# Combining the expert rows by rank: seven ranks read back and added before the end, the eighth tile by tile

## The reference, cut to what matters

```python
def swiglu(x, w1, w3, w2):
    return (silu(x @ w1) * (x @ w3)) @ w2       # 1024 -> 256 -> 1024

def moe(x, ...):
    scores = sigmoid(x @ w_router)
    idx = top 8 of the biased scores within the best 4 of 8 groups
    gates = 2.5 * scores[idx] / sum(scores[idx])
    return swiglu(x, w1_s, w3_s, w2_s) + sum over the 8 of gate * swiglu(x, w1_e[i], w3_e[i], w2_e[i])

x = layer_norm(ALPHA * x + moe(x), ln3_g, ln3_b)
```

## Time and profile before

| | |
|---|---|
| time of the runs, median of 3 | 1402.59 us (1402.55 to 1405.86) |
| span of the profiled execution | 1401.5 us |
| busy: PE, DVE, ACT, POOL | 1282.4, 495.9, 275.4, 226.2 us |
| the first down product ends, the last ends | 588.5 us, 1320.7 us |
| period of an expert within the loop | 11.76 us |

### The profile page before, as it was taken

One profiled execution on the slowest core, in us unless ns is written; L12 is line 12 of the kernel. 1 busy time (PEld: TensorE's weight loads), 2 busy tenths in 40 slices (PEclk: granted clock), 3 DMA queues, 4 the chain that ended last, 5 costly groups with the idle time before them and its releaser, 6 DMA issues.

```text
span 1401.5 us, 19230 instructions
## 1 busy us (share of the span) xinstructions
PE 1282.4 (92%) x7579; PEld 1009.6 (72%) x7579; DVE 495.9 (35%) x1063; ACT 275.4 (20%) x454; POOL 226.2 (16%) x212
## 2 busy tenths in 40 slices
PE   5999596999979999999999999999999999999651
PEld 4888254868846685788888888888888888888420
DVE  0169998131187348111111111111111111111078
ACT  1125124022235150111111111111111111111100
POOL 2039000000000002011111111111111111111061
PEclk9999798999999999999999999999999999999887
DMA  9330303033155532688888888888888888888193
GB/s 340 152 120 2 134 11 150 1 120 136 59 190 233 181 139 69 246 312 318 321 312 313 315 313 310 306 311 308 312 314 315 312 316 311 308 309 305 41 381 160
DMA packets 75990, 319.12 MB, mean 228 GB/s; under 512 B 14055, under 2 KB 20415, under 8 KB 55941
## 3 DMA queue, kind: packets, MB, share of 16 engines
q1 hardware_dynamic: 57525, 278.60, 53.3%
q0 software_dynamic: 16992, 35.49, 7.0%
q10 hardware_dynamic: 1424, 4.35, 0.8%
HBM read 307.16 MB, written 36.38 MB: 245 GB/s over the span
## 4 chain that ended last, share of the span: by engine, by line
PE 77%; DVE 17%; DMA 2%; issue 1%; ACT 1%; POOL 0%; ACTq 0%; DVEq 0%; POOLq 0%; SPq 0%
PE psum L651 73%; DVE act_mem L1461 7%; PE psum L666 5%; DVE act_mem L1921 2%; DMA act_mem<-in_w_conv_b_dram 1%; DVE mk_mem L1621 1%; DVE act_mem L1529 1%; DVE st L1927 1%; DVE act_mem L1932 0%; DMA arena<-in_w_o_dram 0%; DVE act_mem L1915 0%; DVE act_mem L1559 0%; DVE act_mem L1475 0%; DMA arena<-y_rows 0%; DMA y_rows<-act_mem,idx_y 0%
## 5 line engine op out<-in xcount | busy, mean ns | idle before, releaser
L651 PE MATMUL psum<-act_mem,arena 128*128 128x112 f32 (+1 forms) x5504 | 791.6, 305 | 6.7 <-DMA arena<-in_w_o_dram 3.8
L651 PEld LDWEIGHTS psum<-act_mem,arena 128*128 128x128 f32 x5504 | 736.0, 193 | 52.6 <-DMA arena<-in_w_o_dram 4.6
L651 PE MATMUL psum<-arena,act_mem 128*112 128x512 f32 (+2 forms) x616 | 276.7, 593 | 1.0 <-DVE act_mem L1820 0.9
L651 PEld LDWEIGHTS psum<-arena,act_mem 128*112 128x112 f32 (+2 forms) x616 | 101.5, 174 | 124.5 <-issue 123.7
L570 POOL DMA_INDIRECT y_rows<-act_mem,idx_y x64 | 72.6, 1134 | 616.5 <-DVE idx_x L1814 580.4
L1817 DVE TENSOR_TENSOR act_mem<-act_mem,psum 128x224 f32<-128x224 f32 x64 | 24.8, 388 | 389.9 <-ACT act_mem L1351 389.9
L1820 DVE TENSOR_SCALAR act_mem<-psum,act_mem 112x512 f32<-112x512 f32 x64 | 48.0, 750 | 227.9 <-PE psum L651 227.9
L1351 ACT ACTIVATE act_mem<-psum 128x224 f32<-128x224 f32 x64 | 22.9, 358 | 433.3 <-PE psum L651 433.3
L1461 DVE SCALAR_TENSOR_TENSOR act_mem<-act_mem,wcb 128x511 f32<-128x511 f32 (+29 forms) x90 | 86.9, 1016 | 1.1
L1354 ACT ACTIVATE act_mem<-psum,act_mem 112x512 f32<-112x512 f32 x64 | 44.0, 687 | 164.6 <-PE psum L651 164.6
L666 PE MATMUL psum<-ident,act_mem 112*128 112x112 f32 (+4 forms) x390 | 53.5, 280 | 24.8 <-DMA act_mem<-in_x_sample_dram 10.0
(11 more groups left out here) (221 smaller groups left out, 705.9 us busy)
## 6 DMA issues: line engine op xcount, KB each, us to landing
arena<-in_w_e_dram SPq DMA_DIRECT2D x192, 1024.0 KB, 7.9
arena<-in_w_in_dram SPq DMA_DIRECT2D x16, 512.0 KB, 16.9
arena<-in_cache_mem_k_dram SPq DMA_DIRECT2D x8, 1024.0 KB, 9.1
arena<-in_cache_mem_v_dram SPq DMA_DIRECT2D x8, 1024.0 KB, 11.6
arena<-y_rows SPq DMA_DIRECT2D x8, 1024.0 KB, 12.8
arena<-y_rows SPq DMA_DIRECT2D x4, 1536.0 KB, 8.7
arena<-in_w_v_dram SPq DMA_DIRECT2D x1, 4096.0 KB, 24.3
arena<-in_w_k_dram SPq DMA_DIRECT2D x1, 4096.0 KB, 14.0
```

The lines of the kernel that those rows point to most:

```text
L651: return pe.matmul(out, lhsT, rhs, start=first, stop=last)
```

## The change

Instead of reading whole tiles back after the last expert, the kernel reads the rows of one rank for all 512 prompt tokens, as soon as no expert can write that rank any more. Ranks 0 to 3 are read in two halves of two tiles (`early_in`, one buffer for each half, in memory that the router no longer needs) and added by DVE in steps 61 (rank 0), 62 (ranks 1 and 2) and 63 (rank 3). The read of rank 0 stands on SP's queue ahead of expert 63's weights. Ranks 4, 5 and 6 are read into weight slots 0 to 2, and added by DVE, four tiles in one instruction, after its last scaling. Rank 7 is read tile by tile into slot 3. GpSimd's and PE's sums are gone. The 64 rows of the sample tokens are read at the end, and PE sums them with `sel8`, a 0/1 matrix that GpSimd makes at the start. The order of tiles is 0 to 4, the sample tile last, and the statistics of a tile stand before the norm of the tile before it. As the slow path must start from `base` without these sums, SP stores `base` to DRAM at the start of the experts.

```diff
-LAST_ORDER = [4, 0, 1, 2, 3]
-PARTS = [(0, 3), (3, 5), (5, 7), (7, 8)]
-POOL_ROWS = (1, 4)
-PE_ROWS = [(2,), (3,), (5,), ()]
-DVE_ROWS = [(0,), (), (6,), (7,)]
-SMALL_ROWS = [(0, 2), (3,), (5, 6), (7,)]
+NT = SEQ // P
+EARLY = 4
-        y_in = [arena[:, 8192 * n:8192 * n + 8192].rearrange("p (j n) -> p j n", j=TOPK) for n in range(3)]
+        sel8 = sb("sel8", [NS * TOPK, NS])
+        early_in = [kv_mem[:, 2048:4096].rearrange("p (t n) -> p t n", t=2),
+                    act_mem[:, A3:A3 + 2 * D].rearrange("p (t n) -> p t n", t=2)]
+        late_in = [arena[:, 6144 * n:6144 * n + NT * D].rearrange("p (t n) -> p t n", t=NT) for n in range(TOPK - EARLY)]
+        sample_in = kv_mem[0:NS * TOPK, 2048:2048 + D]
+        y_ranks = y_rows[0:SEQ * TOPK, :].rearrange("(t p j) n -> p t j n", p=P, j=TOPK)
-            with sp.Fori(0, E // 4 - 1) as i:
+            wait_out(sp, "so4")
+            for t in range(TT):
+                w = width(t)
+                sp.dma_start(base_rows[t * P:t * P + w, :], base[0:w, t, :]).then_inc(s_bsave, 16)
+            with sp.Fori(0, E // 4 - 2) as i:
                 for n in range(4):
 
                     sp.wait_ge(m_y, 4 * i + (n + 1))
                     expert(n, 4 * i + (n + 4), s_w[n])
 
+            def rank_written(j):
+
+                e = E - TOPK + j
+                sp.wait_ge(m_s[0], 16 * (e // 2 + 1))
+                sp.wait_ge(m_s[1], 16 * ((e + 1) // 2))
+
+            def early_rank(j):
+
+                rank_written(j)
+                for n in range(2):
+                    if j > 0:
+                        sp.wait_ge(s_added[n], j)
+                    sp.dma_start(early_in[n], y_ranks[:, 2 * n:2 * n + 2, j, :]).then_inc(s_early[n], 16)
+
+            for n in range(4):
+                sp.wait_ge(m_y, E - 8 + n + 1)
+                if n == 3:
+                    wait_out(sp, "so4")
+                    sp.wait_ge(s_table, 1)
+                    early_rank(0)
+                expert(n, E - 4 + n, s_w[n])
+            for j in range(1, EARLY):
+                early_rank(j)
             sp.wait_ge(s_over, 1)
+            n_max = sp.value_load(over[0:1, 0:1], min_val=0, max_val=T)
+            for n in range(TOPK - EARLY - 1):
+                sp.wait_ge(m_y, E - 4 + n + 1)
+                rank_written(EARLY + n)
+                sp.dma_start(late_in[n], y_ranks[:, :, EARLY + n, :]).then_inc(s_late_in[n], 16)
+
             sp.wait_ge(m_y, E)
-            n_max = sp.value_load(over[0:1, 0:1], min_val=0, max_val=T)
             with sp.If(n_max > CAP):
+                sp.wait_ge(s_late_add, TOPK - EARLY - 1)
                 with sp.Fori(1, E * (ROUNDS - 1) + 1) as i:
                     sp.wait_ge(f_sem["it"], i)
                     expert(0, (i - 1) % E, f_sem["w"])
-            for p in range(2):
-                sp.wait_ge(m_s[p], 16 * (E // 2))
-            sp.wait_ge(s_done, 1)
-            for n, t in enumerate(LAST_ORDER):
-                w = width(t)
-                if n >= 3:
-                    sp.wait_ge(s_rowv, n - 2)
-                for q, (j0, j1) in enumerate(PARTS):
-                    sp.dma_start(y_in[n % 3][0:w, j0:j1, :],
-                                 y_rows[t * D:t * D + w * TOPK, :].rearrange("(p j) n -> p j n", j=TOPK)[:, j0:j1, :]).then_inc(
-                        s_yin[q][n % 3], 16)
...
+            rank_written(TOPK - 1)
+            for t in range(NT):
+                sp.dma_start(late_in[3][:, t, :], y_ranks[:, t, TOPK - 1, :]).then_inc(s_last_in[t], 16)
+            sp.wait_ge(s_added[0], EARLY)
+            sp.dma_start(sample_in, y_rows[SEQ * TOPK:NROW, :]).then_inc(s_sample_in, 16)
@@ gpsimd @@
+            gp.memset(sel8[:, :], 1.0).then_inc(s_sel8, 1)
+            gp.wait_ge(s_sel8, 1)
+            gp.affine_select(out=sel8[:, :], in_=sel8[:, :], compare_op=ALU.is_ge, fill=0.0, base=0,
+                             pattern=[[-TOPK, NS]], channel_multiplier=1).then_inc(s_sel8, 1)
+            gp.wait_ge(s_sel8, 2)
+            gp.affine_select(out=sel8[:, :], in_=sel8[:, :], compare_op=ALU.is_ge, fill=0.0, base=TOPK - 1,
+                             pattern=[[TOPK, NS]], channel_multiplier=-1).then_inc(s_sel8, 1)
...
-            for n, t in enumerate(LAST_ORDER):
-                w = width(t)
-                rows_in = y_in[n % 3][0:w]
-                gp.wait_ge(s_yin[0][n % 3], 16 * (n // 3 + 1))
-                gp.tensor_tensor(rows_in[:, 0, :], rows_in[:, 0, :], rows_in[:, POOL_ROWS[0], :], ALU.add).then_inc(s_ypool, 1)
-                gp.wait_ge(s_ypool, 2 * n + 1)
-                gp.wait_ge(s_yin[1][n % 3], 16 * (n // 3 + 1))
-                gp.tensor_tensor(rows_in[:, 0, :], rows_in[:, 0, :], rows_in[:, POOL_ROWS[1], :], ALU.add).then_inc(s_ypool, 1)
@@ tensor @@
-            for n, t in enumerate(LAST_ORDER):
-                w = width(t)
-                if w < P:
-                    continue
-                if n >= 4:
-                    pe.wait_ge(s_rowv, n - 3)
-                for q in range(3):
-                    pe.wait_ge(s_yin[q][n % 3], 16 * (n // 3 + 1))
-                    for j in PE_ROWS[q]:
-                        for h in range(2):
-                            last = mm(psum[0:w, n % 4, 512 * h:512 * h + 512], ident[0:w, 0:w],
-                                      y_in[n % 3][0:w, j, 512 * h:512 * h + 512], j == 2, j == 5)
-                last.then_inc(s_ysum, 1)
+            pe.wait_ge(s_sel8, 3)
+            pe.wait_ge(s_sample_in, 16)
+            for h in range(2):
+                last = mm(psum[0:NS, 3, 512 * h:512 * h + 512], sel8[:, :], sample_in[:, 512 * h:512 * h + 512], True, True)
+            last.then_inc(s_ysum, 1)
@@ scalar @@
-            for n, t in enumerate(LAST_ORDER):
+            def last_root(t):
+
+                w, o = width(t), 8 * (t % 2)
+                act.wait_ge(s_var, t + 1)
+                act.activation(small[0:w, o + 2:o + 3], small[0:w, o + 1:o + 2], ACT.Sqrt, bias=eps_t[0:w, 0:1]).then_inc(s_sd, 1)
+
+            last_root(0)
+            for t in range(TT):
                 w = width(t)
-                act.wait_ge(s_var, n + 1)
-                act.activation(small[0:w, 36:37], small[0:w, 35:36], ACT.Sqrt, bias=eps_t[0:w, 0:1]).then_inc(s_sd, 1)
-                dst = o_yp[0, t * P:(t + 1) * P, :] if t < 4 else o_ys[:, 0, :]
-                act.wait_ge(s_res, n + 1)
+                if t + 1 < TT:
+                    last_root(t + 1)
+                dst = o_yp[0, t * P:(t + 1) * P, :] if t < NT else o_ys[:, 0, :]
+                act.wait_ge(s_res, t + 1)
                 act.dma_start(dst, base[0:w, t, :]).then_inc(s_final, 16)
@@ vector @@
+            def add_early(j):
+
+                for n in range(2):
+                    x = base[:, 2 * n:2 * n + 2, :]
+                    if j > 0:
+                        dve.wait_ge(s_added[n], j)
+                    dve.wait_ge(s_early[n], 16 * (j + 1))
+                    dve.tensor_tensor(x, x, early_in[n], ALU.add).then_inc(s_added[n], 1)
+
+            def add_late(n):
+
+                if n == 0:
+                    for m in range(2):
+                        dve.wait_ge(s_added[m], EARLY)
+                else:
+                    dve.wait_ge(s_late_add, n)
+                dve.wait_ge(s_late_in[n], 16)
+                dve.tensor_tensor(base[:, 0:NT, :], base[:, 0:NT, :], late_in[n], ALU.add).then_inc(s_late_add, 1)
+
             for k in range(1, NB):
                 e = NB * LAST + k
                 step(e, k, LAST, 16 * ((e - 1) // 2), 16 * ((e - 5) // 2 + 1))
+                if e == E - 3:
+                    dve.wait_ge(s_bsave, 16 * TT)
+                    add_early(0)
+                if e == E - 2:
+                    add_early(1)
+                    add_early(2)
+                if e == E - 1:
+                    add_early(3)
             y_step(E - 1, NB - 1, 16 * ((E - 1) // 2))
+            for n in range(TOPK - EARLY - 1):
+                add_late(n)
...
+                dve.wait_ge(f_base, 16 * TT)
+                for j in range(TOPK - 1):
+                    if j > 0:
+                        dve.wait_ge(f_add, j)
+                    dve.wait_ge(f_in, 16 * (j + 1))
+                    dve.tensor_tensor(base[:, 0:NT, :], base[:, 0:NT, :], late_in[0], ALU.add).then_inc(f_add, 1)
...
+            dve.wait_ge(s_late_add, TOPK - EARLY - 1)
             dve.wait_ge(s_lnw, 32)
-            for m, t in enumerate(LAST_ORDER):
+            def last_stats(t):
+
                 w = width(t)
-                x = base[0:w, t, :]
-                for q in range(len(PARTS)):
-                    if q == 3 and w == P:
-                        dve.wait_ge(s_ysum, m)
-                        link(dve.tensor_tensor(x, x, psum[0:w, m % 4, :], ALU.add))
-                    if q == 0:
-                        dve.wait_ge(s_ypool, 2 * (m + 1))
-                    else:
-                        dve.wait_ge(s_yin[q][m % 3], 16 * (m // 3 + 1))
```

(51 more changed lines are left out.)

15 lines of the change are left out of this document (12 added, 3 removed).

## The result

The changed kernel takes 1382.08 us (median of 4 runs, 1380.99 to 1383.72), the kernel before 1404.22 in the 4 runs beside it: a ratio of 0.9845, 95% interval 0.983 to 0.986. The forecast was 1377, range 1367 to 1388. The profiled execution took 1383.72 us, the slowest of the four, with a span of 1382.0.

What follows compares the result with a forecast made beforehand. PE bounds the experts; the last 80 us read 17 MB back, add and normalize. Late adds and branch to 1344.5, then 28.7 for the end, 3.1 output: span 1376.3, time 1377.4 (forecast 1377), range 1367 to 1388.

Steps and rivals of the forecast that it cites:

- rank 6: Late reads: issued after scatter 62, taken to land in 8.0 us at 1328.5; rank 6 lands at 1339.7, added to 1344.2.
- the stall of PE: Before the last down product: PE waits for expert 62's scaling behind rank 2's add, starting at 1319.8 instead of 1317.02, 2.7 us.
- the read of rank 2: Steps 62 and 63, two halves on SP's queue: the first lands at 1313.5, the second 2.5 us later, at 1316.
- The end after the adds: Five tiles of sum, statistics and norm on DVE after the late adds: 5.7 us each, 28.7 us in all.
- The branch: Value load and branch between late adds and statistics: 0.3 us, with 3.4 as the far end.
- The output: After DVE's last tile, until the span ends: 3.1 us.
- Hidden edits: Storing base, expert 63's weights behind rank 0's 2 MB, and the sample product: all hidden, cost 0; uncovered, base 5 us.
- Such an add lengthens it by 0.25 and doesn't hold it: GpSimd's scatter starts beside DVE's adds: 0.25 us longer each; were GpSimd held, the time would be 1378 to 1380.
- (a): Rival for the end: DVE alone is the bound, reads land early, stalls stay under a microsecond; 1369 us, chance 0.24.
- (b): Rival for the reads: they come at 3.9 us per MB and scatter 63 lands late; 1385 to 1387 us, chance 0.17.
- (c): Rival for rank reads: 4 KB rows every 32 KB are slower; 1402 us at 5 us per MB, chance 0.05.
- (d): Rival for the end: the adds save nothing because the wait moves; within a few us of before, chance 0.02.

Runs made afterwards that it cites:

- e8: The changed kernel without the storing of base to DRAM, which only the slow path needs: 1382.17 us, against 1382.08 for the changed kernel.
- e1: The changed kernel with SP's read of rank 4 put ahead of rank 3's two halves: 1377.34 us, against 1382.08 for the changed kernel.
- e7: The changed kernel with one more semaphore wait, so the second half of each early rank's add waits for the first half's: 1384.45 us, 1 run.
- e5: The changed kernel with the reads of ranks 2 to 6 spread over weight slots and small buffers as they come free, DVE's adds following: 1374.47 us.
- e2: The changed kernel with ranks 2 and 3 each added one scaling later on DVE: 1383.52 us, against 1382.08 for the changed kernel.
- e4: The changed kernel with all prompt ranks read from one block of 512 rows of x2_rows instead of 4 KB rows every 32 KB: 1381.08 us.
- e10: The changed kernel with reads spread over free buffers, adds of at most 2048 columns with waits between halves, and rank 6 by tiles: 1373.55 us.

## Why the prediction was right, and where it was off

The direction, the range and the order of what binds held: rank 6 was the last to be waited for, and the stall of PE stood where it was forecast. The time was 5.1 us too low (4.7 against the sum's 1377.4), and one term above all was mis-sized, the read of rank 2. By its own steps:

- **The end after the adds.** Forecast 28.7 us, measured 28.4 (1351.32 to 1379.68); tiles 5.67 us apart, forecast 5.7. The adds: 2.29 and 4.43 us, forecast 2.3 and 4.5. The branch: 0.04 us between the last late add (1346.86 + 4.42) and the next sum, forecast 0.3, so it costs nothing more on DVE. The output 2.3, forecast 3.1.
- **Hidden edits.** Storing base costs nothing (e8). Expert 63's weights came in time: the last load is issued at 1286.42 and lands in 11.7 us, as it did before, so rank 0's 2 MB cost the weights far less than the 7.8 us feared, and PE starts on them at 1307.38 without a wait. The sample product lay beside other tiles.
- **The step that was mis-sized** is rank 2: "a lone MB lands 4.8 us after issue, so 1313.5, and the second 2.5 later, 1316". The first half did land in 4.8 us (1310.62 to 1315.44), but the second came 7.9 us after its issue, 5.2 behind the first. With it hd(63) started at 1322.94 instead of 1318.4, which is 2.5 us late when the start's 2.0 are taken off, and SP's reads of rank 3's second half, 4 and 5 moved with it. The stall of PE, forecast as 2.7 us beyond the 0.94 of before, became 5.1. From the issue of rank 3's second half to rank 4's another 1.3 us pass, which was taken as nothing; 0.8 of them are SP's value load and the wait ahead of it, for in e1, where they don't stand between, the step is 0.47. And the reads ran at 325 GB/s from 1324 to 1332, not at 422; that goes with the last 1.3 us. So rank 6 landed at 1346.8 instead of 1339.7: 7.1 us, of which 2.0 are the later start and 5.1 the prediction's.
- **The sum of the miss.** 2.0 (start) + 5.1 (rank 6) - 0.3 (end) - 0.3 (branch) - 0.8 (output) = 5.7, the difference between the span of 1382.0 and the forecast 1376.3. The 2.0 are chance of this execution, and the 0.3, 0.3 and 0.8 are terms that were too dear and happened to help. The runs' times lie 1.7 us above their spans, not 1.1, and the median lies 1.6 below the profiled execution: 5.7 + 0.6 - 1.6 = 4.7, the median's distance from the sum's 1377.4.
- **"Such an add lengthens it by 0.25 and doesn't hold it" was wrong.** GpSimd was held: 4.43, 4.26 and 2.71 us for scatters 60 to 62. The row of before said so, read rightly: a scatter starting 0.34 us ahead of the comparison's end took 1.19, that is 0.34 + 0.85 (the rows stand in the last section), and 0.80 to 0.84 us stand behind the last add in the changed kernel's rows. It didn't matter for the time of the changed kernel (e7 halves the hold and doesn't gain, in its single run), but in e5 it holds rank 6. The prediction had priced it as a side case, at 1378 to 1380 us.
- **Not foreseen:** the stall lowered PE's clock. After 6.02 us of waiting the last product took 6.03 us instead of 3.6. In the changed kernel this lies beside the reads, and e2, where both are gone, is no faster.
- **Rivals.** (a), DVE alone as the bound, came in no run: in e1 the late adds run without a wait, but behind the stall, and the fastest kernels, at 1373.4 and 1373.6, still wait for reads and stay above its 1369. (b) was nearest in kind: for two stretches of 8 us the reads ran at 315 and 325 GB/s, between its 3.9 us a MB (269 GB/s) and the full rate, but from 1332 on it was 419. (c) and (d) are out.

What stays open is why rank 2's second half took 5.2 us behind the first. Scatter 61, released at 1313.57, moves its 0.28 MB between 1315 and 1321, in the midst of that read, and the DMA share falls to 0.64 from 1318 to 1319. But with GpSimd let in earlier (e7) the read still takes 7.1 us, and from another tensor's block (e4) 6.4. No run leaves the scatter out.

## What to carry to other kernels

When work is moved under a stage that is bound by another engine, look at the queue that issues its reads as closely as at the engine that computes: a read that waits for a buffer holds the reads behind it that wait for nothing, and the DMA engines stand partly idle (266 GB/s) just before they become the bound. Removing the visible stall of the main engine gave nothing here; moving one read ahead of a waiting one gave 3 to 5 us, and using every buffer as it came free 7 to 9. Price each half of a double read by what else runs beside it, and take a queue's steps one at a time. When executions differ in their start by more than the gain that is looked for, compare the traces from a point that all kernels share: it takes the chance out of e1's 4.7 us, and shows 2.4 us for e10 that the medians hide.
